# First gathers released by eight picks of one head, its scores moved forward, and the second norm's rows written in two halves

## The reference

```python
def peer_ffn(h, w_query, sub_keys, expert_u, expert_v):
    q = (ht @ w_query).reshape(T, PEER_HEADS, D_KEY)            # 8 heads, 256
    s1 = einsum('thd,kd->thk', q[..., :D_HALF], sub_keys[0])     # 128 scores
    s2 = einsum('thd,kd->thk', q[..., D_HALF:], sub_keys[1])     # 128 scores
    v1, i1 = lax.top_k(s1, 16)
    v2, i2 = lax.top_k(s2, 16)
    cand = v1[..., :, None] + v2[..., None, :]                   # 16 x 16 sums
    sc, ci = lax.top_k(cand, 16)
    e_idx = i1[ci // 16] * N_KEYS + i2[ci % 16]                  # one of 16384 experts
    gate = softmax(sc)
    # per position: w = gelu(expert_u[e] . x) * gate; out = sum w * expert_v[e]
```

## Time and profile before

| what | value |
|---|---|
| time, median of 3 runs | 2996.56 us (2992.25 to 2998.33) |
| the profiled execution's own time | 2996.19 us |
| its span | 2994.5 us |
| busy, share of the span | PE 79%, DVE 66%, ACT 42%, POOL 42% |
| moved by DMA | 1203.87 MB, mean 402 GB/s |
| of it gathers (q0) | 1073.81 MB, 86.9% of 16 engines' span |
| of it other loads (q1) | 127.60 MB, 11.9% |
| chain that ended last, by engine | DMA 49%, PE 28%, DVE 8%, ACT 7%, issue 6%, POOL 2% |

### The profile page before, as it was taken

One profiled execution on the slowest core, in us unless ns is written; L12 is line 12 of the kernel. 1 busy time (PEld: TensorE's weight loads), 2 busy tenths in 40 slices (PEclk: granted clock), 3 DMA queues, 4 the chain that ended last, 5 costly groups with the idle time before them and its releaser, 6 DMA issues.

```text
span 2994.5 us, 38543 instructions
## 1 busy us (share of the span) xinstructions
PE 2372.2 (79%) x12832; PEld 979.0 (33%) x12832; DVE 1982.9 (66%) x4723; ACT 1264.1 (42%) x3737; POOL 1250.1 (42%) x1064
## 2 busy tenths in 40 slices
PE   8778879998986887886886897888797666767665
PEld 6644444544541333232441233234252111111110
DVE  2466737687557766787447866788637777777644
ACT  2136333394434434843333433773434333333333
POOL 0133524343434433454333443554434444455542
PEclk9888989999987998888996899898797666566666
DMA  7899999999999999999999999999999999999997
GB/s 241 307 351 399 412 392 412 402 421 393 416 409 421 415 414 416 421 408 415 417 412 419 412 411 414 409 418 400 419 415 420 420 421 421 421 403 421 421 421 301
DMA packets 226607, 1203.87 MB, mean 402 GB/s; under 512 B 26600, under 2 KB 42472, under 8 KB 95336
## 3 DMA queue, kind: packets, MB, share of 16 engines
q0 software_dynamic: 147456, 1073.81, 86.9%
q1 hardware_dynamic: 78952, 127.60, 11.9%
HBM read 1199.24 MB, written 2.10 MB: 401 GB/s over the span
## 4 chain that ended last, share of the span: by engine, by line
DMA 49%; PE 28%; DVE 8%; ACT 7%; issue 6%; POOL 2%; POOLq 0%; DVEq 0%; ACTq 0%
DMA arena<-in_uv,eidx 42%; PE acc L1345 11%; PE bank L1117 8%; PE bank L1182 8%; DVE arena L1103 5%; DMA unit<-in_w_in 4%; POOL arena L603 2%; DMA unit<-in_w_query 2%; ACT L781 1%; ACT wts L784 1%; ACT L699 1%; ACT diag L790 1%; PE heads L1117 1%; ACT gelu L781 1%; DMA unit<-in_w_out 1%
## 5 line engine op out<-in xcount | busy, mean ns | idle before, releaser
L603 POOL DMA_INDIRECT arena<-in_uv,eidx x1024 | 1214.3, 1186 | 1556.0 <-PE acc L1345 1355.8
L1103 DVE CUSTOM_DVE_ANT_0 arena<-arena,h_nat 128x1024 f32<-128x1024 f32 x1024 | 1255.4, 1227 | 795.5 <-DMA arena<-in_uv,eidx 778.3
L1345 PE MATMUL acc<-arena,diag 64*64 64x512 f32 x8192 | 1382.0, 762 | 469.0 <-ACT diag L790 429.3
L781 ACT ACTIVATE gelu<-dots 128x1 f32<-128x1 f32 x1024 | 206.5, 202 | 1459.0 <-DVE dots L1103 1443.7
L1345 PEld LDWEIGHTS acc<-arena,diag 64*64 64x64 f32 x8192 | 257.0, 154 | 1275.6 <-ACT diag L790 1058.2
L1182 PE MATMUL bank<-hT,unit 128*128 128x256 f32 (+1 forms) x1920 | 397.6, 356 | 27.6 <-DMA unit<-in_w_query 18.9
L790 ACT ACTIVATE diag<-identc,wts 128x64 f32<-128x64 f32 x1024 | 356.1, 348 | 33.6
L1182 PEld LDWEIGHTS bank<-hT,unit 128*128 128x128 f32 x1920 | 306.7, 199 | 193.6 <-issue 148.8
L784 ACT ACTIVATE wts<-gelu,gate 128x1 f32<-128x1 f32 x1024 | 301.4, 294 | 33.2
L1117 PE MATMUL bank<-unit,hT 128*128 128x256 f32 (+1 forms) x640 | 224.6, 487 | 6.4 <-DMA unit<-in_w_out 6.0
L1117 PEld LDWEIGHTS bank<-unit,hT 128*128 128x128 f32 x640 | 114.8, 192 | 130.1 <-issue 115.7
(11 more groups left out here) (130 smaller groups left out, 1400.6 us busy)
## 6 DMA issues: line engine op xcount, KB each, us to landing
unit<-in_w_in SPq DMA_DIRECT2D x55, 1024.0 KB
unit<-in_w_query SPq DMA_DIRECT2D x40, 1024.0 KB
unit<-in_w_out SPq DMA_DIRECT2D x20, 1024.0 KB
arena<-in_uv,eidx POOLq DMA_INDIRECT x1024
x<-in_x SPq DMA_DIRECT2D x4, 512.0 KB, 8.7
out<-hT SPq DMA_DIRECT2D x4, 512.0 KB, 5.2
gain<-in_norm_g SPq DMA_DIRECT2D x2, 512.0 KB
wsp<-in_w_spatial SPq DMA_DIRECT2D x2, 256.0 KB, 16.4
```

The costliest lines, as they stand in the source:

```text
L603: nc.gpsimd.indirect_dma_start(arena[:, n % NBUF, :], None, uv, bass.IndirectOffsetOnAxis(ap=eidx[:, seq % 2, j:j + 1], axis=0)).then_inc( ...
L781: nc.scalar.activation(gelu[:, group], dots[:, group], ACT.Gelu_apprx_tanh).then_inc(s_ge, GROUP)
L1103: V.tensor_tensor_reduce(out=uu, in0=uu, in1=h_nat[:, seq % 3, :], scale=1.0, scalar=0.0, op0=ALU.mult, op1=ALU.add, accum_out=dots[:, n % ...
L1345: ins = nc.tensor.matmul(acc[rows][cols * HALF:(cols + 1) * HALF, :], diag[own, n % NBUF, :], arena[own, n % NBUF, D + f * 512:D + (f + 1) ...
```

## The change

Three edits.

1. The first head of the first tile is picked in two rounds (`first_head`). The first eight of each half, the 64 sums of these, the first eight of those, and their expert numbers, written to `eidx[0:8]`; a new semaphore `s_first` releases GpSimd's slots 0 to 7. Then the second eight of each half, all 256 sums with the first eight picks struck out, the second eight picks and their numbers, `s_idx`. GpSimd waits for `s_idx` at slot 8 as well as at 16. (The eight largest sums of two sorted lists have both places below eight, so the first round's eight are the true first eight.)
2. `unit_scores(0)` is issued inside the pair, after product 19 of 32, in place of after product 22.
3. The second norm's row is written in two instructions of 512 columns, `s_h` counts both, and TensorE waits for each half before its four transposes; the waits on `s_h` elsewhere are doubled.

```diff
@@ SyncE
-                    sp.wait_ge(s_h, first_seq[p])
+                    sp.wait_ge(s_h, 2 * first_seq[p])
@@ GpSimd
-                elif n in (0, K):
+                elif n == 0:
+                    pool.wait_ge(s_first, 1)
+                elif n in (K // 2, K):
                     pool.wait_ge(s_idx, n // K + 1)
@@ VectorE, routing
-                    yield from topk_head(seq, 0, 0)
-                    yield from expert_numbers(l, seq, c, 0, 1)
+                    first_head(l, seq)
                     yield from topk_head(seq, 1, 1)
@@
+            def first_head(l, seq):
+                W = K // 2
+                dve.wait_ge(s_taken, NQ * pass_of[seq] + 1)
+                halves = [(scores[:, seq % 2, f, :], vals[:, f, :], kidx[:, f, :]) for f in range(2)]
+                v, n = top[:, 0, :], tidx[:, 0, :]
+                for s, w, m in halves:
+                    step(V.max(w[:, 0:W], s))
+                    step(V.max_index(m[:, 0:W], w[:, 0:W], s))
+                s = cand[:, 0:W * W]
+                step(V.tensor_tensor(s.rearrange("p (a b) -> p a b", a=W),
+                                     vals[:, 0, 0:W].unsqueeze(2).broadcast_to([P, W, W]),
+                                     vals[:, 1, 0:W].unsqueeze(1).broadcast_to([P, W, W]), ALU.add))
+                step(V.max(v[:, 0:W], s))
+                step(V.max_index(n[:, 0:W], v[:, 0:W], s))
+                eight_numbers(l, seq, 0, W).then_inc(s_first, 1)
+                for s, w, m in halves:
+                    step(V.match_replace(s, w[:, 0:W], s, NEG))
+                    step(V.max(w[:, W:K], s))
+                    step(V.max_index(m[:, W:K], w[:, W:K], s))
+                s = cand
+                step(V.tensor_tensor(...))
+                step(V.match_replace(s, v[:, 0:W], s, NEG))
+                step(V.max(v[:, W:K], s))
+                step(V.max_index(n[:, W:K], v[:, W:K], s))
+                eight_numbers(l, seq, W, K).then_inc(s_idx, 1)
+                dve.wait_ge(s_idx, 1)
+
+            def eight_numbers(l, seq, at, width):
+                W = K // 2
+                sel, self = tsel[:, 0:W], tself[:, 0:W]
+                oh = onehot[:, 0:W * width].rearrange("p (a b) -> p a b", b=width)
+                for half in range(2):
+                    if half == 0:
+                        step(V.tensor_scalar(sel, tidx[:, 0, at:at + W], width.bit_length() - 1, None, ALU.logical_shift_right))
+                    else:
+                        step(V.tensor_scalar(sel, tidx[:, 0, at:at + W], width - 1, None, ALU.bitwise_and))
+                    V.tensor_copy(self, sel)
+                    step(V.tensor_copy(epart[:, half, 0:width], kidx[:, half, 0:width]))
+                    step(V.tensor_tensor(oh, iota ..., self ..., ALU.is_equal))
+                    step(V.tensor_tensor(oh, oh, epart[:, half, 0:width] ..., ALU.mult))
+                    step(V.tensor_reduce(epart[:, half, K:K + W], oh, AX.X, ALU.add))
+                number = epart[:, 0, K:K + W]
+                step(V.scalar_tensor_tensor(out=number, in0=number, scalar=float(KEYS), in1=epart[:, 1, K:K + W],
+                                            op0=ALU.mult, op1=ALU.add))
+                step(V.tensor_scalar(number, number, float(l * NE), None, ALU.add))
+                return V.tensor_copy(eidx[:, seq % 2, at:at + W], number)
@@ VectorE, second norm
-                    V.scalar_tensor_tensor(out=h_nat[:, (q0 + i) % 3, :], in0=x[:, t, :], scalar=r2[:, i:i + 1],
-                                           in1=gain[:], op0=ALU.mult, op1=ALU.mult).then_inc(s_h, 1)
+                    for f in range(2):
+                        cols = slice(f * D // 2, (f + 1) * D // 2)
+                        V.scalar_tensor_tensor(out=h_nat[:, (q0 + i) % 3, cols], in0=x[:, t, cols], scalar=r2[:, i:i + 1],
+                                               in1=gain[:, cols], op0=ALU.mult, op1=ALU.mult).then_inc(s_h, 1)
@@ TensorE, pair
+                                if by_bank and done == total // 2 + 3:
+                                    unit_scores(0)
                                 if part(done, total, 2 * unit_steps(nt)):
@@ TensorE, T2
-                    pe.wait_ge(s_h, q0 + i + 1)
                     for f in range(2):
+                        pe.wait_ge(s_h, 2 * (q0 + i) + f + 1)
                         b = wait_free(pe, p, "T2", i, f)
@@ TensorE, end of dense
-                        if p == 0 and c == 0 and e == unit_steps(nt) + 1:
-                            unit_scores(0)
-                        elif c and e - scores_at(p) in (0, 1) and ...:
+                        if c and e - scores_at(p) in (0, 1) and ...:
```

More of the change, by code:

```diff
@@ L373, in trunk_kernel @@
         s_idx = sem("expert_numbers_ready")
+        s_first = sem("first_expert_numbers_ready")
         s_gates = sem("gates_ready")
@@ L516, in _ @@
                                 load_x(t)
-            sp.wait_ge(s_h, first_seq[NP])
+            sp.wait_ge(s_h, 2 * first_seq[NP])
             sp.dma_start(gain[:], final_g.rearrange("(a d) -> a d", a=1).broadcast_to([P, D])).then_inc(s_gain, 16)
@@ L834, in routing @@
                                 dn.unsqueeze(2).broadcast_to([P, HC, K]), ALU.mult).then_inc(s_gates, 1)
+            def first_head(l, seq):
[18 more added lines that the diff above has]
+                s = cand
+                step(V.tensor_tensor(s.rearrange("p (a b) -> p a b", a=K),
+                                     vals[:, 0, :].unsqueeze(2).broadcast_to([P, K, K]),
+                                     vals[:, 1, :].unsqueeze(1).broadcast_to([P, K, K]), ALU.add))
+                step(V.match_replace(s, v[:, 0:W], s, NEG))
[3 more added lines that the diff above has]
+                dve.wait_ge(s_idx, 1)
@@ new lines, in eight_numbers @@
+            def eight_numbers(l, seq, at, width):
[9 more added lines that the diff above has]
+                    step(V.tensor_copy(epart[:, half, 0:width], kidx[:, half, 0:width]))
+                    step(V.tensor_tensor(oh, iota[:, 0:width].unsqueeze(1).broadcast_to([P, W, width]),
+                                         self.unsqueeze(2).broadcast_to([P, W, width]), ALU.is_equal))
+                    step(V.tensor_tensor(oh, oh, epart[:, half, 0:width].unsqueeze(1).broadcast_to([P, W, width]), ALU.mult))
+                    step(V.tensor_reduce(epart[:, half, K:K + W], oh, AX.X, ALU.add))
[4 more added lines that the diff above has]
+                return V.tensor_copy(eidx[:, seq % 2, at:at + W], number)
@@ L1316, in dense @@
                         e += 1
-                        if p == 0 and c == 0 and e == unit_steps(nt) + 1:
-                            unit_scores(0)
-                        elif c and e - scores_at(p) in (0, 1) and (p, c - 2 + e - scores_at(p)) != (0, 0):
+                        if c and e - scores_at(p) in (0, 1) and (p, c - 2 + e - scores_at(p)) != (0, 0):
                             unit_scores(c - 2 + e - scores_at(p))
```

## The result

| | before | after |
|---|---|---|
| time, median of 18 runs | 2997.96 us (2990.57 to 3004.70) | 3006.18 us (2997.92 to 3014.93) |
| ratio | | 1.0028, 95% interval 1.0018 to 1.0037 |
| span of the profiled execution | 2994.5 us | 3005.1 us |

The change makes the kernel 8.2 us slower (5.4 to 11.1 by the interval). Forecast was +4.5 us, 3001.1, with a range of 2994 to 3006: the direction and the main mechanism hold, the size is short, and the time lies just above the range.

What follows compares the result with a forecast made beforehand. The prediction took the DMA engines' stream of gathers, full from about 160 us, as the bound. A first dot product 5.0 us later, less 0.5 in later tiles, made 2996.6 + 4.5 = 3001.1 us, range 2994 to 3006.

Steps and rivals of the forecast that it cites:

- (1): Second norm in halves: first query product 0.5 us earlier (0.3 to 0.7), and 0.5 us gained in later tiles.
- (3): First eight picks on VectorE: path to their numbers takes 5.54 us in place of 10.57, so 5.03 us earlier.
- (4): Query-weight loads among earlier gathers: three loads slowed, last landing at 138.4 us, first dot product 5.0 us later.
- rival A: Start of first pass: loads starved by gathers, last half at the high clock, +4.5 us; chance 0.54 together with E.
- B: Same starved loads, but PE at the low clock when the last half begins: +7.2 us, chance 0.25.
- D: Gathers' head start reaches the dot products whole, gates not waiting for the last load: -6.2 us, chance 0.04.
- E: Narrow picks cost as much as wide ones, so a 4.5 us head start: +3.8 us, chance counted within A's 0.54.
- C: Queued loads hold their own against gathers, last load landing 0.5 us earlier: -1.0 us, chance 0.15.
- Step 5: From first dot product to the end: DMA is full from 160 us, so the 5.0 us delay carries whole.

Runs made afterwards that it cites:

- e1: Kernel before plus only the picks in two rounds, norm and scores as before: 3004.70 us, 1.0026 of the kernel before.
- e6: Changed kernel with query weights laid out so a load has 8 KB pieces, not 2 KB: 2982.64 us, 0.9962 of the kernel before.
- e7: Kernel before with all 115 unit loads in 8 KB pieces and forget weights in one piece per partition: 2956.61 us, ratio 0.9867.
- e2: Kernel before plus only the norm in halves and the moved scores, picks as before: 2993.95 us, 0.9995 of the kernel before.
- e8: Norm in halves and moved scores, picks as before, first gather held until the last query-weight load landed: 2994.65 us, 0.9988 of the kernel before.
- e4: Kernel before with the first gather held until the last load of query weights landed: 2992.33 us, ratio 0.9988.
- e9: Kernel before with five extra VectorE instructions ahead of the first gates, loads and first gathers untouched: 3003.84 us, ratio 1.0020.
- e3: Changed kernel with the third gather held until the last load of query weights landed: 2996.56 us, 1.0003 of the kernel before.
- e5: Kernel before with query weights laid out so a load has 8 KB pieces, not 2 KB: 2982.03 us, ratio 0.9956.
- e10: Changed kernel with all unit loads in 8 KB pieces and forget weights in one piece per partition: 2956.54 us, 0.9861 of the kernel before.
- e11: Norm in halves and moved scores, picks as before, all unit loads in 8 KB pieces: 2955.16 us, 0.9856 of the kernel before.

## Why the prediction was wrong, and where it was right

All times from the norm; predicted ones are those of the prediction less 86.34.

| step | predicted | measured |
|---|---|---|
| (1) first query product | 3.0 | 3.10 |
| (3) path to the first eight numbers | 5.54 | 5.41 |
| first gather issued | 17.4 | 17.49 |
| its data starts | 19.7 | about 22 |
| of the five late loads, moved by then | 2.10 MB | 2.91 MB |
| (4) rate of a load among gathers | 0.093 MB/us | 0.090 (1.98 in 22 us) |
| moved among all nine gathers | 2.70 MB in 29 us | 2.28 in 28 (115 to 143 us) |
| from the last bytes to the start of the last half | 2.0 | about 3 (143.0 to 145.99) |
| second half of the third pair there | 33.0 | 32.85 (e1: 28.04) |
| first half of the last pair there | 44.3 | 45.01 (e1: 40.59) |
| last load there | 52.1 | 52.99 (e1: 52.39) |
| its 32 records | 3.7, high clock | 3.84, high clock |
| from there to the first dot product | 1.2 | 1.5 |
| first dot product | 57.0 | 58.36 |

**Right.** What bounds the start, the head start of the first gather's issue, that loads among the gathers decide, the turn for each packet, and the direction. The turns are seen as equal numbers of packets while both queues have work, whatever the two carry: 452 to 452 in the earlier trace rows and 51 to 51 in its first microsecond alone, 986 to 985 in the changed kernel from 120 to 142 us, 194 to 198 in e6 and 342 to 342 in e7. In the changed kernel's first four, 115 to 119 us, it is 168 packets of gathers to 112 of loads. VectorE's idle time was forecast at some 21 us and is 21.73: the head of picks that is now finished later costs nothing. The norm in two instructions took 1.42 us for 1.28, where 0.1 more was forecast. The last half did meet the high clock, after a pause of 1.13 us, so rival A and not B is what the profiled execution shows, but e1 shows B at the same place: with 6.04 us, after a pause of 5.76. D is refuted by the profile; E did not happen, the head start was 6.1 us. C is refuted by the change's own profile and by e1: the last load is there 8.6 and 8.0 us later from the norm, not 0.5 earlier. A piece of C holds all the same: the loads that stood in the queue before the gathers' data kept the engines (2.91 MB moved, not 2.10).

**The step that failed is (4), in its sizes.** It put the delay of the first dot product at 5.0 us, by three whole loads among the gathers from 106.0 us on. The delay is 6.4 us (7.9 in e1, with the low clock). And the way there was another: the gathers' data starts 2.3 us later from the norm than forecast, so only 2.3 MB of load meet it and not 3.15. But these move slower as a whole (2.28 MB in 28 us, 0.20 of it in the first four), and landing takes about 3 us and not 2. That the last load is there within 0.9 us of the forecast is partly luck, since these errors cancel. So is the match for the third pair's second half, 32.85 for 33.0: e1, by the same picks, has it at 28.04, and in the changed kernel's profile PE was held up at 118 to 122 us in a way that e1 doesn't show (see the end). The other 0.5 us lie in the last 32 records and the way to the first dot product.

**How the miss adds up.** From 3001.1 to 3006.18 there are 5.1 us. 1.4 are the base: I had the median of 3 runs before, 2996.56, and 18 runs have 2997.96. 1.4 are the first dot product, 6.4 for 5.0. 0.5 is what I took off for the norm's halves in later tiles: no run shows that gain, e2 as a whole is 0.9995 with an interval across 1, and e8 is no better than e4. The remaining 1.8 no run assigns. With 6.4 us carried whole, as e9 allows (6.0 of 6.6, between 2.4 and 9.6), the sum would have been 3003; the measured 8.2 us (5.4 to 11.1) includes 6.4.

**The range was too narrow above.** I let its upper edge stand at 3006, near the upper end of the rival with the low clock, while the medians of the kernel before alone moved by 2 us between groups of runs (2995.53 to 2997.96) and the executions of one kernel spread over 14 to 17 us. B (7.2) may have deserved more than 0.25: of the two kernels with early picks, narrow loads and no gather held, one shows it.

**Step 5 holds on one side only.** A first dot product 6.4 or 6.6 us later costs about as much at the end (the change, e9). One that is 11.6 us earlier (e4) gives 3.6. One that is 9.7 us earlier (e3) gives nothing that can be measured. In e4 VectorE then waits for gathers; for e3 the cause is open.

**Open.** Whether the remaining 1.8 us between 6.4 and 8.2 are noise, the low clock of rival B in part of the executions, or the low clock ahead of the norm occurring more often by chance in one kernel's runs than in the other's: one profile for each kernel can't tell how often either occurs.

## What to carry to other kernels

A head start for a stream of long packets (over 7 KB here) was paid here by the loads of short packets (2 KB) that were issued after it: look for what waits for those loads before releasing the stream, and count packets, not bytes. Where both are needed, try packets for the loads as long as those of the stream. Here 8 KB pieces of the query weights made the change harmless (e5, e6), and 8 KB pieces of all unit loads made the kernel 40 us faster, most of it by less engine time for the same bytes (e7, 319 us for 356). A transfer that starts earlier is worth nothing when its consumer waits for something else, and an earlier consumer gained little here once it waited for the transfer (e4).

## What the runs showed of the hardware that I had not expected

The spread of times was smaller in the kernels whose loads have fewer packets (22632 in all in e7, 78952 in the kernel before): executions of the kernel before lie between 2987 and 3005 us, the four of e7 between 2954.71 and 2957.59, those of e10 between 2955.1 and 2957.02, those of e11 between 2953.91 and 2956.87. But it is not the query weights alone: with only these in long pieces the spread stays (e5 2975.40 to 2989.34, e6 2975.99 to 2992.30). None of the three profiles with all loads wide has the stretch at the low clock ahead of the norm, against 4 of the other 10. With four executions of each kernel this is a hint, and what the spread comes from no run shows.

PE at the low clock through a window of 19 us with 18.14 us of work in it (57 to 76 us above) is one of four such stretches in 13 profiled executions. The second norm starts at 89.82 to 93.00 us in the four and at 84.63 to 86.97 in the others.

In two of the 13 traces, the kernel before and the changed one, other engines see late what PE releases, while GpSimd issues its first nine gathers. In the changed kernel ScalarE's copy of scores waited 8.34 us for a release that the profile can't name, though PE's two score products for it were done by 118.4 us. SyncE issued the last load 2.2 us after PE had finished the half before (121.6 to 123.82); in e1 that took 0.03 us. PE itself worked in single records with pauses of 1.04 and 0.46 us from 119.6 us on. In the kernel before the same happened until 122.8 us: two copies of ScalarE's waited 4.50 and 5.38 us, and SyncE's unit load issued at 122.83 waited 8.3. The other eleven traces have no such wait from 96 to 146 us, though eight of them issue the same run of gathers. So the gathers alone are not the cause; what is, no run shows. It cost little here: e1, without it, has its last load there only 0.6 us sooner from the norm.

```profile
123.58 0.66 ACT L734 ACTIVATE scores<-heads 128x256 f32<-128x256 f32 x2 [8.34 <-remote]
```
